# Gate and up products of experts 0, 1 and 2 one behind the other, ahead of the table of lists and the first down product

## What is computed

```python
scores = sigmoid(x @ router_w)
_, idx = top_k(scores + router_bias, 8)
wsel = sel / sum(sel) * 2.5                        # gates[n, e]
hid = silu(einsum('nd,edf->nef', x, exp_w_gate)) * einsum('nd,edf->nef', x, exp_w_up)
routed = einsum('nef,efd->nd', hid * gates[..., None], exp_w_down)
x = x + g_f * (routed + shared)
```

## Time and profile before

| | us |
|---|---|
| median of three runs | 778.68 |
| lowest and highest | 777.18, 780.59 |
| the profiled execution | 780.85 |
| its span | 778.8 |
| PE busy | 689.0 (88%) |
| DVE busy | 329.9 (42%) |
| POOL busy | 304.9 (39%) |
| ACT busy | 222.6 (29%) |
| mean rate of all DMA | 359 GB/s |

### The profile page before, as it was taken

The page is one execution under the profiler, slowest core; times in us unless marked ns, Lnnn a source line. Parts: engine busy times, 40 slices in busy tenths (PEclk is TensorE's granted clock), DMA queues, the critical chain, the costliest instruction groups (busy, mean ns, idle before and its releaser), DMA issues.

```text
span 778.8 us, 14944 instructions
## 1 busy us (share of the span) xinstructions
PE 689.0 (88%) x5081; PEld 386.2 (50%) x5082; DVE 329.9 (42%) x613; ACT 222.6 (29%) x380; POOL 304.9 (39%) x322
## 2 busy tenths in 40 slices
PE   4999999998999999999999999997899878988910
PEld 3666556454555554455555565553455434544500
DVE  4161668378544424443333433333334334233326
ACT  4034602132233311232223323232223223223202
POOL 0050112114155644356436544464446554363220
PEclk9999999999999999999999999999999999999975
DMA  8997999864799999999999999999999999999752
GB/s 354 424 334 284 370 408 362 357 248 164 257 345 375 397 411 393 390 392 389 398 380 387 395 396 398 391 404 404 412 414 395 394 405 412 402 400 402 280 145 86
DMA packets 59517, 279.49 MB, mean 359 GB/s; under 512 B 19027, under 2 KB 19391, under 8 KB 32072
## 3 DMA queue, kind: packets, MB, share of 16 engines
q1 hardware_dynamic: 36112, 252.72, 79.9%
q0 software_dynamic: 23136, 25.28, 13.5%
q10 hardware_dynamic: 216, 0.79, 0.3%
HBM read 272.83 MB, written 26.30 MB: 384 GB/s over the span
## 4 chain that ended last, share of the span: by engine, by line
PE 70%; DMA 19%; DVE 5%; issue 2%; SPq 1%; ACT 1%; POOL 0%; POOLq 0%; DVEq 0%; ACTq 0%
PE bank L1115 31%; PE bank L1151 15%; DMA gu<-in_exp_w_up 14%; PE bank L856 4%; PE bank L874 4%; PE bank L977 4%; PE bank L1091 3%; DMA gu<-in_lru_in_w 3%; PE bank L844 2%; PE bank L1132 2%; PE bank L1208 1%; DMA sh<-acc_rows 1%; PE bank L1087 1%; PE bank L877 1%; PE bank L1060 1%
## 5 line engine op out<-in xcount | busy, mean ns | idle before, releaser
L1115 PE MATMUL bank<-gu,et 128*64 128x256 f32 x2480 | 289.3, 387 | 23.6 <-DMA gu<-in_exp_w_up 19.2
L1115 PEld LDWEIGHTS bank<-gu,et 128*64 128x64 f32 x2480 | 183.3, 139 | 145.0 <-issue 69.5
L565 POOL DMA_INDIRECT acc_rows<-et,idx x64 | 104.1, 1627 | 239.2 <-DVE et L1648 141.1
L1151 PE MATMUL bank<-dn,et 128*64 128x512 f32 x632 | 149.7, 602 | 12.3 <-issue 10.1
L1641 DVE COPY et<-bank 128x256 f32<-128x256 f32 x64 | 27.2, 424 | 254.2 <-PE bank L1132 254.2
L751 ACT ACTIVATE et<-bank 64x512 f32<-64x512 f32 x64 | 37.9, 592 | 262.5 <-PE bank L1115 262.5
L1151 PEld LDWEIGHTS bank<-dn,et 128*64 128x64 f32 x632 | 40.4, 136 | 79.2 <-issue 79.2
L761 ACT ACTIVATE et<-bank,mb 128x512 f32<-128x512 f32 x64 | 44.0, 687 | 118.1 <-PE bank L1151 101.7
L1648 DVE TENSOR_SCALAR et<-bank,mb 128x512 f32<-128x512 f32 x64 | 48.1, 751 | 67.3 <-PE bank L1151 57.7
L1634 DVE TENSOR_TENSOR et<-et 64x512 f32<-64x512 f32 x64 | 67.8, 1060 | 0.4 <-ACT et L752 0.4
L575 POOL DMA_DIRECT2D small<-halfc x49 | 55.7, 1138 | 0.0
(11 more groups left out here) (290 smaller groups left out, 600.0 us busy)
## 6 DMA issues: line engine op xcount, KB each, us to landing
dn<-in_exp_w_down SPq DMA_DIRECT2D x64, 1024.0 KB, 23.6
gu<-in_exp_w_up SPq DMA_DIRECT2D x63, 1024.0 KB, 24.6
gu<-in_exp_w_gate SPq DMA_DIRECT2D x62, 1024.0 KB, 21.4
gu<-in_ada_rest SPq DMA_DIRECT2D x5, 2048.0 KB, 10.1
gu<-in_mix_w SPq DMA_DIRECT2D x3, 2048.0 KB, 13.9
mb<-in_ada_rest SPq DMA_DIRECT2D x3, 2048.0 KB, 11.6
gu<-in_lru_in_w SPq DMA_DIRECT2D x4, 1024.0 KB, 17.3
gu<-in_sgu_in_w SPq DMA_DIRECT2D x2, 2048.0 KB, 19.6
```

The costliest lines, as they stand in the source:

```text
L565: pool.indirect_dma_start(acc_rows[u % 2], bass.IndirectOffsetOnAxis(ap=idx[:, u, 0:1], axis=0), yo[:, u % 2, 0, :], None, bounds_check=2 ...
L1115: mm = pe.matmul(bank[u % 2][64 * c:64 * c + 64, b * FE:(b + 1) * FE], xt[:, b, k % 4, k // 4, :], w[c][:, k * FE:(k + 1) * FE], start=(k ...
L1151: mm = pe.matmul(bank[5 + b][64 * c:64 * c + 64, :], hT[:, b, j, :], dn[:, dslot(u), j * D + c * HALF:j * D + (c + 1) * HALF], start=(j == ...
```

## The change

On PE the gate and up products of experts 0, 1 and 2 follow each other with only the turning of tokens and hidden rows between them. Behind that of expert 2 stand table products 0 to 3, turn h of 1, turn x of 3, table products 4 to 7 and down 0. Behind the gate and up of expert 3 stand down 1, turn h of 2, turn x of 4 and down 2. DVE and ACT are reordered to match: the sums, the spread and the indices of experts 4, 5 and 6 move from step 1 (and 2) to step 2, `y0` and `y1` of expert 0 behind them, those of expert 1 to step 3. On SP the gate and up of expert 7 now stand ahead of the down of expert 4, those of expert 8 ahead of the down of expert 5. No instruction is added or taken away, and POOL's program is the same.

```diff
@@ SP
             load_gu(0, 0, SLOTS + 2)
+            load_gu(0, 0, SLOTS + 3)
             load_dn(0, 0, SLOTS)
-            load_gu(0, 0, SLOTS + 3)
+            load_gu(0, 1, 0)
             load_dn(0, 0, SLOTS + 1)
-            load_gu(0, 1, 0)
@@ ACT, body
-                    if first and r == 0 and u == 1:
-                        spread_table(0)
+                    front = first and r == 0
+                    if front and u == 3:
+                        y1(0, 0, 1)
                     if not (last and u == U - 1):
                         xt1(r, i + (u + 1) // U, (u + 1) % U)
-                    if not (first and u == 0):
+                    if front and u == 2:
+                        spread_table(0)
+                        y1(0, 0, 0)
+                    elif not (first and u == 0 or front and u == 1):
                         y1(r, i if u else i - 1, (u - 1) % U)
@@ PE, body
+                    front = first and r == 0
                     gate_up(r, i, u, now)
...
-                    if first and r == 0 and u == 0:
+                    if front and u == 2:
                         table(0, 0)
-                    if first and r == 0 and u == 1:
-                        table(0, 2)
+                        table(0, 1)
+                    if front and u == 3:
+                        down(0, 0, 1, full_1)
                     if before is not None:
                         turn_h(r, i if u else i - 1, (u - 1) % V, before)
...
-                    if first and r == 0 and u == 0:
-                        table(0, 1)
-                    if before is not None:
+                    if front and u == 1:
+                        full_0 = before
+                    elif front and u == 2:
+                        full_1 = before
+                        table(0, 2)
+                        down(0, 0, 0, full_0)
+                    elif before is not None:
                         down(r, i if u else i - 1, (u - 1) % V, before)
@@ DVE, body
+                    front = first and r == 0
+                    if front and u == 2:
+                        moving(0, 2)
+                        xt0(0, 0, 3)
+                        hidden(0, 0, 2)
+                        table_sums(0)
+                        for e in range(FIRST, FIRST + 3):
+                            index(0, 0, e)
+                        ht(0, 0, 1)
+                        y0(0, 0, 0)
+                        continue
+                    if front and u == 3:
+                        y0(0, 0, 1)
                     if not (first and u == 0):
                         ht(*before)
-                    if first and r == 0 and u == 1:
-                        table_sums(0)
...
                     hidden(r, i, u)
-                    if late and u == 0:
-                        moving(0, 2)
-                    if late and u == 1:
-                        index(r, 0, FIRST)
-                        index(r, 0, FIRST + 1)
-                    if not (first and u == 0):
+                    if not (first and u == 0 or front and u == 1):
                         y0(*before)
```

More of the change, by code:

```diff
@@ L1659, in body @@
                         shared_turned(half // 2)
-                    late = first and r == 0 and u < 2
+                    late = front and u < 2
                     if not (late or last and u >= U - AHEAD - 1):
```

## The result

| | before | after |
|---|---|---|
| median, us | 779.29 | 788.95 |
| lowest and highest | 777.18, 780.59 | 787.87, 790.33 |
| profiled execution | 780.85 | 790.33 |
| its span | 778.8 | 788.3 |

The changed kernel is slower: 1.0123 times the time of before, interval 1.0105 to 1.0141, or 9.7 us. The prediction was 780.6 us with a range up to 784.5. The direction, slower, was forecast; the size, 9.7 us where 1.9 was forecast, is beyond every case that I had named.

The account below looks back on a forecast made before the run. The DMA engines were taken as the bound from 226 us. Counting holes gave 1.6 us of lag, counting work done 2.4; taking 1.9 on the median of 778.68 gave 780.6 us, range 775.5 to 784.5.

Parts of the forecast that it names:

- What bounds the kernel: From 226 us the DMA engines, at share 1.03 and 398 GB/s; only idle DMA time before that counts.
- Gate and up 1 and 2: Copies of xt end last; gate and up start at 207.1 and 212.7, and load of 7 goes at 216.3.
- The hole ahead of the down of 4: New DMA hole from 223.0 to 227.3 us, 3.7 us after allowing for the gather of 4.
- The stall near 240: PE waits about 1.8 us (0 to 3) for the gather of 5, as one stall with the scatter of 0.
- the faster rival: Holes before 226 us are closed, giving 774.2 to 776.1 us; chance 0.10.
- No hole: Queued loads, gathers and scatters last to 246.4 us; the down load of 7 could start at 244.3, 2.1 us in hand.
- PE's delay costs nothing, 5.4 us in hand: At the queue's thinnest place, 333.74 us, 5.4 us are in hand, so PE's delay of 4.6 us costs nothing.
- The rule that was weighed: With 435 GB/s reachable, 37 GB/s is free after 226 us; lag is caught up within 22 us, time unchanged.
- my sum of holes: Idle DMA time until the queue stays full: 5.3 us before, 6.9 after, so 1.6 us behind.
- The slower one: PE's delay empties the queue at 244 and 333 us, giving 783.3 to 785 us; chance 0.14.
- Copies hold: Copies of xt hold gate and up of 2 beyond 216 us, up to 2.9 us, 781.6; chance 0.08.

Follow-up runs that it names:

- e10_late12: Kernel before with 82 dummy transposes on PE ahead of gate and up of expert 32; 779.04 us, 1.0002 times before.
- e6_delay12: Kernel before with 82 dummy transposes on PE ahead of gate and up of expert 9; 788.24 us, 1.0129 times before.
- e1_fill: Changed kernel with 14 dummy products on PE in the two gaps behind the copies of xt for experts 1 and 2; 786.85 us.
- e2_gather5: Changed kernel with the gather of expert 5 put ahead of the scatter of expert 0 on POOL; 790.63 us.
- e8_free: Changed kernel with gathers of 5 and 6 ahead of scatter of 0, gather of 7 ahead of scatter of 2, own result buffers for 2 and 3; 790.12 us.
- e11_warm: Changed kernel with 27 dummy transposes on PE between turn h of 3 and turn x of 5; 784.34 us.
- e12_down0_again: Second run of the program that moves only down of 0, with its y0 and y1, behind gate and up of 2 in the kernel before; 783.66 us.
- e5_delay4: Kernel before with 27 dummy transposes on PE ahead of gate and up of expert 9; 781.05 us, 1.0035 times before.
- e7_down0: Kernel before with only down of 0, and its y0 and y1, moved behind gate and up of 2, table left in place; 784.45 us.
- e9_table: Changed kernel with the down product of 0 back at its old place, so that the table is moved without it; 784.91 us.

## Why the prediction was wrong, by its own steps

**What bounds the kernel: right.** The end follows the DMA queue: PE 9.2 us later at 473 us costs 0.1 us (e10_late12), the same at 266 us costs 9.1 (e6_delay12), and in every profile of the table the lag at 350 us is PE's delay at expert 19 less 0.9 to 1.3 us.

**Gate and up 1 and 2: sizes slightly off.** PE started 0.55 us behind the end of ACT's copy, where I had allowed 0.2 (the copy at 207.26 took 0.60 us, gate and up began at 208.41). In this profile, gate and up of 0 also ended 0.9 us late, and gate and up 1 ran at a granted clock of 0.50 from 209 to 212 us, 5.36 us in place of 3.67. The load of 7 went at 219.88, not 216.3; without those two chances it would have been at 217.3.

**The hole ahead of the down of 4: right in place and kind.** The down of 4 went at 229.2 (forecast 225.85), 9.3 us behind the load of 7 (9.55). The kernels with the same load order and no slow gate and up 1 or late start (e1_fill, e2_gather5, e8_free, e11_warm) lag 2.3 to 3.3 us at 240 us, against my 1.6 to 2.4. Against the 1.9 us that I took, this term was undersized by 0.4 to 1.4 us, in the profiled execution by 3.8, of which 2.6 are the two chances above.

**The stall near 240: mis-sized.** I had 1.8 us, with 3 as the other end; it was 4.5. The gather of 5 was issued at 235.14 (231.2 forecast, PE having been 3.3 us late) and PE went on at 246.1, 11.0 us later, where I had taken the 8.8 us of the earlier trace rows. The scatter of 0 held `y1` to 242.8: 11.5 us from the start of its first part, 9.5 from that of its second, where the earlier trace rows have 11 from a second part and I had 239 to 240. The two waits didn't end together, as I had it, but 3.3 us apart; that removing one leaves the other is what e2_gather5 shows.

**The fall of the clock: not in the prediction at all.** After the wait the granted clock was 0.53 (the 1.2 GHz level and a little of the 2.4 GHz one) from 246 to 249 us; turn x and down 3 took 1.11 and 3.11 us in place of 0.66 and 1.94, together 1.6 us. I had a row that shows it, gate and up behind a wait in 5.36 us, and used it only for the faster rival. The Trainium skill, page "TensorE: Matmul & The Clock Gate", section "HAM oscillation — how this bites in real kernels", says that a PE that has waited for a DMA starts its next products cold; the traces agree for the longest waits (3.11 us behind a wait of 4.51, 3.52 behind 4.51 in e1_fill, 3.57 behind 3.19) and for 1.94 us behind 1.02. In between they go either way. Two rows, of e10_late12 and of e11_warm, show gate and up at full clock behind waits as long as that of e12_down0_again:

```profile
714.41 3.67 PE L1115 MATMUL bank<-gu,et 128*64 128x256 f32 x32 [3.30 <-DMA gu<-in_exp_w_up]
```
```profile
720.73 3.67 PE L1119 MATMUL bank<-gu,et 128*64 128x256 f32 x32 [3.39 <-DMA gu<-in_exp_w_up]
```

**"No hole" behind it: the step that failed first.** The down load of 7 was to be issued at 242.85 with 2.1 us in hand. PE finished down 3 at 250.3, 7.5 us later than forecast: 3.3 carried from before, 2.6 of the longer wait, 1.6 of the clock. The queue ran out at 248 us, share 0.22, and 3.9 us of lag came between 240 and 262 us, where the sum had nothing. With the stall removed (e8_free) this loss is 0.7.

**"PE's delay costs nothing, 5.4 us in hand": the step that was wrong in kind.** What is in hand is far less. e5_delay4 and e6_delay12 lose 2.6 and 8.2 us of lag between 262 and 350 us, at a delay that exceeds the lag at 262 us by 3.6 and 9.5 us (6.4 less 2.8, 10.7 less 1.2), so 1.0 to 1.3 us is in hand; e8_free gives 1.2 by the same count (7.5 less 6.3). The reading was wrong because I took the time from SP's next issue to the landing of the last load. In e6_delay12 such a load lands late beside scatters and a gather, and with no other load queued the rate is down to half well before it lands (202 GB/s from 322 us, landing at 325.5), and the next load, issued at 325.88, brought the rate back only near 328 us (221 GB/s from 327 to 328, 410 from 328 to 330). Half of 3.5 us and the 0.6 us by which the start takes longer than the 1.4 that I allowed make 2.4 of the 4.1 us by which I overstated it; where the rest lies is open. In the changed kernel itself this step cost 0.9 us, as its delay at expert 19 exceeds the lag at 262 us by 2.1 (11.7 less 9.6); but it let the sum treat PE's delay as free, where it counts nearly in full.

**The terms together.** Forecast: 1.9 us of lag by 240 us, none after it. Measured in the profile: 5.7 by 240, 3.9 to 262, 0.9 to 350, 10.5 us in all. The term that failed most is the one that I had put at nothing, what PE's delay does to the queue after 240 us: 4.8 us, and 4.6 in e1_fill, whose profile has neither of the two chances.

**The rule that was weighed.** The Trainium skill, page "Perfetto Trace Analysis", section "Roofline", gives about 435 GB/s as what the DMA engines of one active core can reach. The estimate worked out from it, that the lag would be caught up with what is left below that rate, fails here: both kernels move 398 to 399 GB/s from 262 to 732 us, and a lag of 9.6 us at 262 us is still 10.5 us at 725, where the same bytes are compared. What the page says in "Identifying the Most-Contended Engine", that occupancy misleads for DMA and that the rate should be read, this case confirms: a share of 0.92 went with 202 GB/s, and a share of 1.03 with 398. The same fault was in my sum of holes: by share (1.03 less the share, from 205 to 262 us) the changed kernel left 14.6 us idle and before 6.6, 8.0 us more, or 8.8 counted from 190 us; by bytes the lag is 9.6.

**The rivals.** The slower one had the mechanism (POOL and the scatters late, waits for gather and scatter, queue empty at 244). Its price of 4.6 us at 9 us of delay counted 5.4 us as in hand; with 1.3 us in hand, 9 us of delay would be 7.7, and the 11.7 that were measured 10.4, beside a measured lag of 10.5. The "faster" rival needed the down of 0 ended before 222.5; it ended at 229. "Copies hold" came true in this profile by its two chances (gate and up 2 started at 216.17); without them it started at 213.6 to 213.8 against 212.7, worth 1 us.

**What isn't settled.** Why e2_gather5 is slower by its median (12.0) than by its lag (10.9), beyond that its profile is of its fastest execution (788.48 us, median 790.63); how often gate and up 1 is slow in the changed kernel; when the clock falls behind a wait of 1.8 to 3.4 us and when not; and how the 5 us of e7_down0 divide between the wait, the clock and the order of loads. No kernel that I tried is faster than the one before.

## What to carry to other kernels

How much delay a queue of loads can take is read from the rate, not from the landing of the last load nor from the share: find the place where GB/s falls, and put a known delay of dummy work into the kernel before the change to measure it. A reordering that makes something small and early later (lists, a gather, a scatter) pays the full latency of a small transfer in a full queue, 8.4 to 11.8 us here, once for each link of the chain (in e8_free the scatter of 0, then that of 2 behind it). Before moving work "to where the engine waits", look whether it waits there at all: PE had 0.3 us idle in the 21 us that this change rearranged.

## What the hardware showed that I had not expected

- A wait of 4.5 to 6 us on PE cost itself and then made what followed slow, each of the six times: granted clock near 0.5 for the next 3 to 7 us, a down product at 3.1 to 3.7 us in place of 1.94, in e8_free a gate and up at 5.36 in place of 3.67. Waits of 1.0 and 1.3 us did not do it. In between it went either way: 1.83 us was followed by a low clock in one profile and not in five others, 1.94 us by a gate and up of 5.36 us (e12_down0_again at 559 us), 2.16, 2.68 and 3.19 us by slow down products, and 3.30 and 3.39 us by a gate and up at full clock.
- Dummy transposes in such a wait made the kernel faster, 784.34 against 788.95 us.
- Where one load at most was queued and scatters were under way, the DMA engines stood at a share of 0.94 to 1.11 with 154 to 225 GB/s (e6_delay12, 310 to 314 and 322 to 324 us).
- Small indirect transfers beside queued loads of 1 MB: the gather of 5 released PE 11.0 us behind its issue (10.9 in e1_fill, whose row names it), and the scatter of 0 released `y0` or `y1` 8.4 to 11.8 us behind the start of its second part (e9_table, e2_gather5; 9.5 in the changed kernel).
